# Macaron block in fp32: 18 of 22 up-projection tiles by seven half-size products, two periods deep, instead of 12

## What is computed

```python
D_FF = ((8 * D_MODEL // 3 + 255) // 256) * 256      # 2816 = 22 tiles of 128

def swiglu(x, wgu, wd):
    gate, up = jnp.split(x @ wgu, 2, axis=-1)
    return (jax.nn.silu(gate) * up) @ wd
...
    for i in range(DEPTH):
        h = h + 0.5 * swiglu(rms_norm(h, ffn1_norm[i]), ffn1_wgu[i], ffn1_wd[i])
        ...
        h = h + 0.5 * swiglu(rms_norm(h, ffn2_norm[i]), ffn2_wgu[i], ffn2_wd[i])
```

## Time and profile before

| | |
|---|---|
| median of 3 runs | 2158.29 us (2158.24 to 2161.63) |
| the profiled execution | 2159.57 us, its span 2157.6 us |
| PE busy | 2120.6 us, 98% of the span |
| DVE busy | 1511.3 us, 70% |
| ACT busy | 907.7 us, 42% |

### The profile page before, as it was taken

One profiled execution on the slowest core, in us unless ns is written; L12 is line 12 of the kernel. 1 busy time (PEld: TensorE's weight loads), 2 busy tenths in 40 slices (PEclk: granted clock), 3 DMA queues, 4 the chain that ended last, 5 costly groups with the idle time before them and its releaser, 6 DMA issues.

```text
span 2157.6 us, 30026 instructions
## 1 busy us (share of the span) xinstructions
PE 2120.6 (98%) x12251; PEld 1852.7 (86%) x12251; DVE 1511.3 (70%) x2194; ACT 907.7 (42%) x1305; POOL 140.9 (7%) x114
## 2 busy tenths in 40 slices
PE   8999999999999999999999999999999999999998
PEld 6788888888888889889888888988898888898887
DVE  7877776657654787767687777757686457877774
ACT  6433434335444443434353333344454345334332
POOL 0000002100020200000010000021001101000001
PEclk9999999999999999999999999999999999999999
DMA  4333332422221233333323333343132212432331
GB/s 142 113 108 103 89 108 88 137 93 84 98 98 59 78 110 99 103 104 103 99 77 118 100 111 93 98 137 98 65 113 98 79 60 86 123 103 89 108 103 54
DMA packets 267940, 211.96 MB, mean 98 GB/s; under 512 B 7358, under 2 KB 234268, under 8 KB 267804
## 3 DMA queue, kind: packets, MB, share of 16 engines
q1 hardware_dynamic: 264544, 205.55, 30.7%
q10 hardware_dynamic: 3260, 4.51, 0.8%
HBM read 207.93 MB, written 2.10 MB: 97 GB/s over the span
## 4 chain that ended last, share of the span: by engine, by line
PE 87%; DVE 8%; ACT 3%; issue 2%; ACTq 0%; POOL 0%; POOLq 0%; DVEq 0%
PE ps L1816 22%; PE ps L1817 22%; PE ps L1818 21%; PE ps L2023 7%; PE ps L2025 7%; PE ps L2024 7%; DVE w_lo L1118 1%; DVE ex L1682 1%; DVE mx L1662 1%; ACT ex L997 1%; ACT w_hi L641 1%; DVE hn_lo L1131 1%; DVE Gn L1269 0%; DVE Gn L1265 0%; DVE form_lo L1338 0%
## 5 line engine op out<-in xcount | busy, mean ns | idle before, releaser
L1816 PE MATMUL ps<-hid_hi,wn_hi 128*128 128x512 f32 x592 | 232.6, 393 | 2.4 <-DVE wn_lo L1362 1.8
L1817 PE MATMUL ps<-hid_lo,wn_hi 128*128 128x512 f32 x592 | 231.3, 391 | 0.0
L1818 PE MATMUL ps<-hid_hi,wn_lo 128*128 128x512 f32 x592 | 230.4, 389 | 0.0
L1373 DVE SCALAR_TENSOR_TENSOR h<-ps,h 128x512 f32<-128x512 f32 x224 | 148.3, 685 | 83.6 <-PE ps L1818 80.7
L1817 PE MATMUL ps<-hn_lo,wn_hi 128*128 128x512 f32 x448 | 175.2, 391 | 0.0
L1816 PE MATMUL ps<-hn_hi,wn_hi 128*128 128x512 f32 x448 | 175.1, 391 | 0.0
L1818 PE MATMUL ps<-hn_hi,wn_lo 128*128 128x512 f32 x448 | 174.2, 389 | 0.0
L641 ACT ACTIVATE w_hi<-raw 128x2048 fp32r<-128x2048 f32 x61 | 116.7, 1914 | 118.9 <-PE ps L1818 98.9
L1816 PE MATMUL ps<-hn_hi,w_hi 128*128 128x512 f32 x384 | 151.7, 395 | 2.0 <-DVE w_lo L1175 2.0
L1818 PE MATMUL ps<-hn_hi,w_lo 128*128 128x512 f32 x384 | 150.3, 391 | 0.0
L1817 PE MATMUL ps<-hn_lo,w_hi 128*128 128x512 f32 x384 | 150.2, 391 | 0.0
(11 more groups left out here) (323 smaller groups left out, 5900.6 us busy)
## 6 DMA issues: line engine op xcount, KB each, us to landing
raw<-in_ffn_wgu_dram SPq DMA_DIRECT2D x174, 512.0 KB, 4.7
raw<-in_ffn_wd_dram SPq DMA_DIRECT2D x48, 512.0 KB, 3.8
raw<-in_ffn_wd_dram SPq DMA_DIRECT2D x80, 256.0 KB, 3.7
raw<-in_w_in_dram SPq DMA_DIRECT2D x40, 512.0 KB, 4.5
raw<-in_cross_wkv_dram SPq DMA_DIRECT2D x32, 512.0 KB, 3.9
raw<-in_w_out_dram SPq DMA_DIRECT2D x16, 512.0 KB, 4.0
raw<-in_cross_wq_dram SPq DMA_DIRECT2D x16, 512.0 KB, 3.9
raw<-in_cross_wo_dram SPq DMA_DIRECT2D x16, 512.0 KB, 4.0
```

Source lines behind the costliest of these rows:

```text
L1373: dve.scalar_tensor_tensor(out=h[:, m, :], in0=ps[:, down_bank(c, m), :], scalar=0.5, in1=h[:, m, :], op0=ALU.mult, op1=ALU.add).then_inc( ...
L1816: pe.matmul(dst, a_hi, b_hi, start=start, stop=False)
L1817: pe.matmul(dst, a_hi, b_lo, start=False, stop=False)
L1818: return pe.matmul(dst, a_lo, b_hi, start=False, stop=stop)
```

## The change

Tiles 0 to 3 stay whole, and tiles 4 to 21 are all fast. There are 18 periods of one fast tile each. In period n, PE does step 1 of tile n, step 4 of tile n-1, then steps 2 and 3 of tile n, then steps 5 and 6 of tile n-1, with eight down products (four in periods 1 to 3) in three gaps between. A chunk of three tiles now spreads over three periods. Three bank pairs rotate for the fast tiles, and down results share two banks. The weight forms of a fast tile are two sets: the first (`form_hi`, `form_lo`: two plain blocks, two sums) is made one period ahead, the second (`more_hi`, `more_lo`: one plain block, two sums) at the end and at the start of periods.

```diff
-FAST = 12
+FAST = 18
...
+    order = [("N", 0), ("N", 1), ("N", 2), ("DA", 0), ("DB", 0), ("N", 3), ("DA", 1),
+             ("S", 0), ("S", 1), ("DB", 1), ("S", 2), ("S", 3)]
+    for c in range(2, CHUNKS - 1):
+        q = 3 * c - 2
+        order += [("DA", c), ("S", q), ("S", q + 1), ("DB", c)]
+        if q + 2 < FAST:
+            order.append(("S", q + 2))
+    return order + [("DA", CHUNKS - 1), ("DB", CHUNKS - 1)]
...
+    if n == 0:
+        gaps = [[(0, 0), (1, 0)], [(0, 1), (1, 1)], []]
+    elif n < 4:
+        gaps = [[(2 * n, 0), (2 * n, 1)], [(2 * n + 1, 0)], [(2 * n + 1, 1)]]
+    else:
+        i = 8 * ((n - 4) % 3)
+        gaps = [[divmod(i + a, 3) for a in range(*ab)] for ab in ((0, 3), (3, 6), (6, 8))]
...
-                def form_plain(q):
-                    u = up + FFN_AT["S", q]
-                    dve.wait_ge(form_rounded, 3 * (fast_no(F, q) - 1) + 1)
-                    dve.tensor_tensor(out=form_lo[:, q % 2, 512:2048], in0=raw[:, u % 2, 512:2048],
-                                      in1=form_hi[:, q % 2, 512:2048].bitcast(f32), op=ALU.subtract).then_inc(w_split, 1)
...
+                def first_plain(q):
+                    u = up + FFN_AT["S", q]
+                    dve.wait_ge(first_rounded, 2 * (fast_no(F, q) - 1) + 1)
+                    dve.tensor_tensor(out=form_lo[:, q % 2, 0:1024], in0=raw[:, u % 2, 1024:2048],
+                                      in1=form_hi[:, q % 2, 0:1024].bitcast(f32), op=ALU.subtract).then_inc(first_forms, 1)
...
+                def second_plain(q):
+                    u = up + FFN_AT["S", q]
+                    dve.wait_ge(second_rounded, 2 * (fast_no(F, q) - 1) + 1)
+                    dve.tensor_tensor(out=more_lo[:, q % 2, 1024:1536], in0=raw[:, u % 2, 512:1024],
+                                      in1=more_hi[:, q % 2, 1024:1536].bitcast(f32), op=ALU.subtract).then_inc(w_split, 1)
...
+                for n in range(FAST):
+                    c, r = gap_products(n)[0], (n - 4) % 3 if n >= 4 else None
...
+                    if r == 0:
+                        down_split(c, 1)
...
+                    second_plain(n)
+                    if n >= 2:
+                        fast_product_(n - 2)
+                    second_sums(n)
+                    if n >= 2:
+                        hid_low(fast_tile(n - 2), G[:, n % 2, :])
+                    if n:
+                        gate0(n)
+                    gate0_scale(n)
+                    if n:
+                        up1(n - 1)
+                    add_gap(n, 0)
+                    if n + 1 < FAST:
+                        first_plain(n + 1)
+                        form_sums(n + 1)
+                    add_gap(n, 1)
+                    if n + 1 < FAST:
+                        first_sums(n + 1)
...
+                    if r == 1:
+                        down_split(c, 3)
+                    if r == 2:
+                        down_split(c + 1, 0)
+                    if n:
+                        gate1(n - 1)
+                        up0(n - 1)
+                        fast_scale(n - 1)
+                    add_gap(n, 2)
+                    if r == 0:
+                        down_split(c, 2)
...
-                late_unit(3, range(KT))
-                for j in range(ROUNDS):
-                    q, c = 2 * j, j + 1
...
+                third_unit()
+                for n in range(FAST + 1):
+                    if n < FAST:
+                        fast_step(n, 1)
+                    if n:
+                        fast_step(n - 1, 4)
+                    gap(n, 0)
+                    if n < FAST:
+                        fast_step(n, 2, 3)
+                    gap(n, 1)
+                    if n:
+                        fast_step(n - 1, 5, 6)
+                    gap(n, 2)
                 last_chunk()
```

More of the change, by code:

```diff
@@ L437, in wn_no, with down_bank, pair @@
         def wn_no(F, n):
-            return F * 20 + n
+            return F * 14 + n
         def wn_rounded_no(F, n):
-            return F * 40 + n
+            return F * 28 + n
+        def down_bank(c, m):
+            if c in (0, CHUNKS - 1):
+                return 4 * (c > 0) + m % 4
+            return 4 + m if c == 1 and m < 4 else 6 + m % 2
+        def pair(q):
+            return 2 * ((q + 1) % 3)
         def quarter_at(p, tiles):
-            return p * 512 if tiles == 2 else (p % 2) * 768
+            return (0, 512, 1024, 0)[p] if tiles == 2 else (p % 2) * 768
         def quarter(w, p, tiles):
@@ L1278, in whole_low @@
                 def whole_low(i):
[L1279 removed]
+                    hid_low(i, Gn[:, :])
                 def fast_low(q):
@@ L1351, in whole_split @@
-                def whole_split(i, part):
-                    u = up + FFN_AT["N", i]
-                    dve.wait_ge(wn_rounded, wn_rounded_no(F, (7 + 6 * (i - 4) if i > 3 else 1) + part))
-                    c = (slice(0, 768), slice(768, 2048))[part]
-                    dve.tensor_tensor(out=wn_lo[:, c], in0=raw[:, u % 2, c], in1=wn_hi[:, c].bitcast(f32), op=ALU.subtract)\
-                       .then_inc((wn_ready, w_split)[part], 1)
+                    dve.wait_ge(first_rounded, 2 * (fast_no(F, q) - 1) + 1)
@@ L1374, in add_part, with add_gap @@
                                              op0=ALU.mult, op1=ALU.add).then_inc(d_read, 1)
+                def add_gap(n, gap):
+                    c, ends = gap_ends(n, gap)
+                    for m in ends:
+                        add_part(c, m)
                 def add_last(m):
@@ L1491, in ffn @@
                 dve.tensor_tensor(out=w_lo[:, 1, 0:1536], in0=raw[:, u % 2, 0:1536], in1=w_hi[:, 1, 0:1536].bitcast(f32),
-                                  op=ALU.subtract).then_inc(w_split, 1)
+                                  op=ALU.subtract)
+                gate1(FAST - 1)
+                up0(FAST - 1)
+                fast_scale(FAST - 1)
+                fast_product_(FAST - 1)
+                add_gap(FAST, 2)
+                down_split(CHUNKS - 1, 1)
+                hid_low(fast_tile(FAST - 1), G[:, (FAST - 1) % 2, :])
                 def after_add(m):
@@ new lines, in gap @@
+                    for m, t in gaps[g]:
+                        p = m // 2
+                        if t == 0:
+                            if c == 1 and m < 2:
+                                pe.wait_ge(n_read, whole_no(F, 2))
+                            elif c == 1 and m < 4:
+                                pe.wait_ge(n_read, whole_no(F, 3))
+                            elif m >= 2:
+                                pe.wait_ge(d_read, d_read_no(F, c, m - 2))
+                            else:
+                                pe.wait_ge(d_read, d_read_no(F, c - 1, m + 6))
+                            if m % 2 == 0:
+                                if p % 2 == 0:
+                                    pe.wait_ge(wn_ready, wn_no(F, 2 * c + p // 2))
+                                else:
+                                    wait_split("DA" if p == 1 else "DB", c)
+                        if m == 0:
+                            pe.wait_ge(hid_ready, hid_no(F, tiles[t]))
+                        a = quarter_at(p, len(tiles)) + t * 256 + (m % 2) * P
+                        last = down_tile(down_bank(c, m), tiles[t], (wn_hi[:, a:a + P], wn_lo[:, a:a + P]),
+                                         t == 0, t == len(tiles) - 1)
+                        if t == len(tiles) - 1:
```

536 lines of the change are left out of this document (228 added, 308 removed).

## The result

| | before | changed |
|---|---|---|
| median | 2158.32 us (2158.24 to 2161.63, 4 runs) | 2267.72 us (2266.96 to 2269.36, 4 runs) |
| ratio | | 1.0503, 95% interval 1.049 to 1.0516 |
| span of the profiled execution | 2157.6 us | 2265.0 us |

The changed kernel is 109 us slower. The direction was forecast, the size was not: 2221 us, and the range ended at 2248.

What follows compares the result with a forecast made beforehand. PE bounds the kernel before; after the change the load loop does, 48.4 us a round against 45.17 of PE work. +15.4 a stage, +62 in four, plus 2 at stage changes, on 2159.57 gives 2223, median 2221; range 2190 to 2248.

Steps and rivals of the forecast that it cites:

- What bounds the kernel, and PE's saving: PE's own pace bounds a round of 46.52 us; the change takes 1.35 us off it, leaving 45.17.
- What it asks of DVE: DVE's work in a round of three periods: 38.5 of 45.2 us, so it fits.
- The loop through the load: Fast tile buffer's release to next release, through load, ACT and DVE: 15.4 to 16.6 us a period, 48.4 a round.
- I take 4.95, with a hand-over of 0.03, so 4.98: Time of a fast tile's weight load within the loop, from buffer release: 4.98 us.
- Both bounds: Limits on the load: at 4.4 us, 2190 us in all; at 5.2, about 4 us longer.
- The next stage's first weights: At stage changes, loaded after the last chunk's second split, split between last adds: 0.7 us in three stages, 2 in all.
- From one such release to the next, PE plays no part: Between successive releases of the fast tile buffer, PE adds nothing to the loop's 15.4 to 16.6 us.
- Rival 2: The loop plus PE's clock falling to 1.2 GHz after waits: 30 us more, 2257 us; 8 in 100.
- Rival 1: The load hides and PE stays the bound: 2150 us, or 2126 with entry and exit waits hidden; 7 in 100.
- Rival 3: DVE and ACT slower side by side, losing 0.08 us overlap per DVE instruction: 2270 us at most; 10 in 100.
- The range: Total time from 2190 us, with the load at 4.4, to 2248, taking in part of rivals 2 and 3.

Runs made afterwards that it cites:

- the small load: Changed kernel with only the first 128 of 1024 depth rows of each fast tile's weights loaded: 2180.05 us.
- The exit's order alone: Changed kernel with only the next stage's first weights rounded and split after the second result of the last chunk: 2263.43 us.

## Why the prediction was right or wrong

**What bounds the kernel, and PE's saving: right.** The work fell as counted, 8.1 us a stage by PE's starts. A round in which PE does not wait takes 45.67 us with the small load, 0.5 above the forecast's 45.17, so a round saves 0.85 us and not 1.35.

**"What it asks of DVE": right.** 39.6 us of DVE's busy time in a round hinder nobody, since with the small load the same work stands in a round of 45.67.

**"The loop through the load": the mechanism right, its main term mis-sized.** Release to release goes through load, ACT, splits, sums and gate, as forecast. Each part was tested by itself: the load later (+110 us), smaller (-88), the sums ahead of ACT's rounding (-70), the release earlier (-41). The terms behind the load were good: in the second periods they make 10.46 us, where the forecast has 15.4 - 4.98 = 10.4, and in the first and third 0.3 and 0.1 more than it had.

The step that failed is "I take 4.95, with a hand-over of 0.03, so 4.98". I took it from the GB/s, where most of the bytes are in; what ACT waits for is the landing of the second DMA. The trace of before had that time for this very load, and I read the earlier trace rows wrongly. The row of the two DMAs lasts 0.99 us, the second issue 0.58 of it, so the second starts 0.41 us after the first and not 0.6. And the median of 4.5 mixes first DMAs, which landed after 3.8 to 4.2 us, with second ones, which took 4.7 to 5.5. For the load issued at 176.73 alone:

```profile
L484 SPq DMA_DIRECT2D raw<-in_ffn_wgu_dram x2: 368/476/584, 176.7 to 177.1; - x2
...
DMA to landing us min/median/max: 3.8/4.3/4.9
```

0.4 and 4.9 make 5.3 us. In the whole kernel before, the 28 loads of fast tiles were complete 5.41 us after their issue in the mean (5.18 to 6.05). In the changed kernel 5.41 were measured up to ACT's start. So the load takes what it took before; only now somebody waits for it. At 70 us for each us of load, the 0.43 missing are 30 of the 46.5 us. (By periods it is the same: 1.25 us in each of 16 rounds are 20, and the loads of the second to fourth fast tile of each stage, at 5.85 in place of 4.98, are 10.)

Both bounds failed with it. The 4.4 adds the shortest landing of a first DMA to the 0.6, and the 5.2 lies under the mean. I had kept the landing of 5.5 out because "the loop issues one at a time". That was false (191.05 and 192.09), and so was what I said of the 5.5: it belongs to the load issued at 269.77, and the nearest others before and after it were issued at 258.47 and 276.74. With the down loads cut to an eighth the load still took 5.35.

**The next stage's first weights: too small.** Forecast were 0.7 us in each of three stage changes. The exit's order alone gave back 4.3 us. The omitted step: ACT too stands still for the late load, and behind it the low parts of `h`.

**"From one such release to the next, PE plays no part": not quite.** DVE waited in the loop for PE at L1341 (`up0`, late behind a slow stretch) 16 times, 10.8 us in all, and 3.4 us in four waits at L1335 (`gate1`). Such waits may be the 0.45 us by which a round's terms behind the load were too short, 7 us in 16 rounds. But only 1.8 us were given back when the clock was kept up, which is within the spread of the runs, so this part is argued from the trace and not shown. Load, exit and these 7 us make some 41 of the 46.5; the rest stays open.

Rival 2 had the fall right and its price too high: it added 30 us in full for PE's clock, in a kernel where PE had time.

**The rivals.** Rival 1 (the load hides) did not come about; with the load made small, the time was 2180, not its 2150, since, by my estimate, six rounds of 0.5 us more than forecast are 3 us a stage, which leaves some 4 us a stage for entry and exit beyond what it had. Rival 3 (slower instructions) did not either: DVE's starts lie 1.14 us apart for 1024 elements (214.90 to 216.04), where the forecast had 1.13 from the kernel before.

**The range.** It was made from one span of the load, 4.4 to 5.2, with a small part for the clock. Load and exit both err to the same side, and the true load lay outside the span.

## What to carry to other kernels

When a transfer gets into a loop, its price is the time from the issue to the consumer's start, landing of the last DMA included, and it is multiplied by every turn of the loop: here 0.43 us became some 30. Read that time for one load at a time, not from a bandwidth curve or from a median over the DMAs of a pair, which land at different times. To shorten such a loop, look for work between the landing and the release that can stand elsewhere; moving one instruction of DVE gained 70 us, a second 41, and together they brought PE back as the bound. And do not take idle or slow time of an engine that is not the bound for the cause: keep it busy there and see whether the total moves.

## What the runs showed of the hardware

- A load of 1 MB in two DMAs takes 5.41 us from issue to use (mean of 56), and 4.78 us for three quarters of the bytes. In the kernel before, where nobody waited for it, it was complete after 5.41 us too (mean of 28). DMAs of 64 KB each land after 1.9 us, of 448 KB after 4.3, of 512 KB after 4.7; of the pairs of 512 KB for fast tiles in the kernel before the first landed after 3.7 to 4.6 us and the second after 4.7 to 5.6.
- Waits of about 2 us inside a round mostly let the clock of PE fall: after one of 2.12 us it was at 1.2 GHz from 1.7 us after PE's restart, for 3.3 us. It fell behind 12 of the 20 waits at this place; in the round from 241.2 to 290.6 it stayed at 1.00 behind one of 1.94 us. With 1.36 us of such a wait filled with matmuls, it fell once in the rounds of the whole kernel.
